# A mixture-of-experts weight ring: the first three tiles of each next unit are issued inside the running unit, and five tiles move back from idle arrays into the ring

## The reference, cut to what matters

```
logits = (xt @ w_router)
top_v, top_i = lax.top_k(logits, TOP_K)                  # TOP_K = 2
gate = sum(one_hot(top_i, N_EXPERTS) * softmax(top_v)[..., None], axis=1)
for e in range(N_EXPERTS):                               # 8 experts, D = 1024, D_FF_EXPERT = 2816
    out = out + gate[:, e:e+1] * ((silu(xt @ wg[e]) * (xt @ wu[e])) @ wd[e])
```

## Time and profile before

| | before |
|---|---|
| median of 3 runs | 1498.73 us (1493.27 to 1499.72) |
| the profiled execution, its own time | 1498.9 us |
| its span, first to last instruction | 1497.0 us |
| PE busy | 1433.6 us, 96% of the span |
| DVE, ACT busy | 529.7 us, 303.5 us |
| DMA, mean over the span | 276 GB/s |
| DMA in the experts' part | some 417 GB/s where it is busy throughout |
| chain that ended last | PE 91% |

### The profile page before, as it was taken

One profiled execution on the slowest core, in us unless ns is written; L12 is line 12 of the kernel. 1 busy time (PEld: TensorE's weight loads), 2 busy tenths in 40 slices (PEclk: granted clock), 3 DMA queues, 4 the chain that ended last, 5 costly groups with the idle time before them and its releaser, 6 DMA issues.

```text
span 1497.0 us, 60951 instructions
## 1 busy us (share of the span) xinstructions
PE 1433.6 (96%) x27147; PEld 1274.0 (85%) x27147; DVE 529.7 (35%) x1496; ACT 303.5 (20%) x870; POOL 38.7 (3%) x59
## 2 busy tenths in 40 slices
PE   5999999999999999999999899999999999999997
PEld 3888588999547787888778899999999999999896
DVE  1474427666636355788623210000101010010012
ACT  2112423000102523455342010100101010000101
POOL 0100000000000000100000000000000000000000
PEclk9999999999999999999999999999999999999999
DMA  9823849544448132100185999999999999999995
GB/s 390 321 95 123 308 170 396 196 170 169 179 180 330 57 127 87 35 8 7 48 283 219 378 397 403 417 417 418 399 418 399 419 417 417 417 403 417 394 414 212
DMA packets 77441, 413.76 MB, mean 276 GB/s; under 512 B 12920, under 2 KB 13354, under 8 KB 40452
## 3 DMA queue, kind: packets, MB, share of 16 engines
q1 hardware_dynamic: 68752, 399.96, 67.4%
q0 software_dynamic: 7456, 9.56, 2.2%
q10 hardware_dynamic: 1108, 2.41, 0.4%
HBM read 407.50 MB, written 6.48 MB: 277 GB/s over the span
## 4 chain that ended last, share of the span: by engine, by line
PE 91%; DVE 3%; DMA 2%; ACT 2%; issue 1%; ACTq 0%; DVEq 0%; SPq 0%
PE banks L1691 29%; PE banks L1715 14%; PE banks L1070 9%; PE banks L1109 4%; PE banks L718 3%; PE banks L721 3%; PE banks L824 3%; PE banks L827 3%; PE banks L1236 2%; PE banks L1295 2%; PE banks L744 2%; PE banks L1656 1%; PE banks L1313 1%; PE banks L860 1%; PE banks L1324 1%
## 5 line engine op out<-in xcount | busy, mean ns | idle before, releaser
L1691 PE MATMUL banks<-w,ring 128*64 128x86 f32 x11072 | 450.2, 238 | 8.1 <-issue 5.1
L1691 PEld LDWEIGHTS banks<-w,ring 128*64 128x64 f32 x11072 | 426.6, 136 | 18.9 <-issue 7.5
L3216 DVE TENSOR_TENSOR w<-w,banks 128x86 f32<-128x86 f32 x176 | 43.1, 245 | 566.5 <-PE banks L1691 558.4
L1715 PE MATMUL banks<-w,ring 128*64 128x86 f32 x5568 | 237.2, 238 | 1.7 <-issue 1.5
L1715 PEld LDWEIGHTS banks<-w,ring 128*64 128x64 f32 x5568 | 219.4, 137 | 2.0 <-issue 2.0
L2252 ACT ACTIVATE w<-banks 128x86 f32<-128x86 f32 x176 | 42.7, 242 | 587.7 <-PE banks L1691 587.7
L718 PE MATMUL banks<-w,ring 128*128 128x256 f32 x224 | 49.2, 380 | 0.6 <-issue 0.3
L744 PE MATMUL banks<-ring,ct 128*32 128x256 f32 x768 | 47.3, 395 | 2.3 <-ACT ct L1818 2.1
L721 PE MATMUL banks<-ring,w 128*128 128x256 f32 x224 | 48.9, 379 | 0.0
L718 PEld LDWEIGHTS banks<-w,ring 128*128 128x128 f32 x224 | 42.3, 190 | 7.4 <-issue 1.8
L721 PEld LDWEIGHTS banks<-ring,w 128*128 128x128 f32 x224 | 42.3, 190 | 5.9 <-DVE w L2334 0.2
(11 more groups left out here) (481 smaller groups left out, 1747.2 us busy)
## 6 DMA issues: line engine op xcount, KB each, us to landing
ring<-in_moe_gu SPq DMA_DIRECT2D x173, 1024.0 KB, 12.1
ring<-in_moe_w_down SPq DMA_DIRECT2D x174, 512.0 KB, 12.2
ring<-in_ada_w SPq DMA_DIRECT2D x48, 1024.0 KB, 5.2
ring<-in_ev_w_in SPq DMA_DIRECT2D x11, 1024.0 KB, 27.1
ring<-in_ffn_w_gate SPq DMA_DIRECT2D x11, 1024.0 KB, 12.4
ring<-in_ffn_w_up SPq DMA_DIRECT2D x11, 1024.0 KB, 10.8
ring<-in_ffn_w_down SPq DMA_DIRECT2D x11, 1024.0 KB, 6.4
ring<-in_ev_w_out SPq DMA_DIRECT2D x4, 1024.0 KB, 6.8
```

The lines of the kernel that those rows point to most:

```text
L1691: ins = [mm(b[hp, 0:CAP], w[:, k, hp], XG[:, k, :], start=k == 0, stop=k == KC - 1, skip_group_check=True) for hp in HALVES]
L1715: ins = [mm(bank[4 + c // 4][hp, (c % 4) * CAP:(c % 4 + 1) * CAP], w[:, c * P + hp.start:c * P + hp.stop], HIDU[:, t % 2, :], start=t == 0 ...
L3216: v.tensor_tensor(HIDU[:, t % 2, :], SILU[:, t % 2, :], bank[2 + t % 2][:, 0:CAP], ALU.mult).then_inc(sem("hid"), 1)
```

## The change

It has three parts. (1) SP's order: after d4, d5 and d6 of a unit, SP issues gu0, gu1 and d0 of the following unit, each behind a wait for the use of the same tile in the running unit. They no longer stand at the unit's end. Unit 7 issues none. (2) `AHEAD` is gone: in unit 0 the five tiles go through the ring like all others, and PE's unit 0 uses the same hardware loop as the others. (3) SP reads the running and the following unit's expert from the table `TBL` in each unit from 1 on; before, it did so only for the last.

```diff
-UNIT_TILES = [("gu", 0), ("gu", 1), ("d", 0)]
+FIRST_TILES = [("gu", 0), ("gu", 1), ("d", 0)]
+UNIT_TILES = []
...
+EARLY = {("d", ROWS): (("gu", 0), up_taken(0)), ("d", ROWS + 1): (("gu", 1), up_taken(1)),
+         ("d", ROWS + 2): (("d", 0), down_taken(0))}
...
-        AHEAD = {("gu", ROWS + 2 + n): W[6 + n][:, :] for n in range(3)}
-        AHEAD.update({("d", ROWS + 1 + n): W[9][:, n * D:(n + 1) * D] for n in range(2)})
...
-                    if u is None and (kind, b) in AHEAD:
-                        sp.wait_ge(sem("x"), 6)
-                        sp.dma_start(AHEAD[kind, b], src).then_inc(sem("x_in"), 16)
-                        continue
...
-            expert_tiles(None, 0)
-            with sp.Fori(1, NE - 1) as u:
-                expert_tiles(u, u)
+            def expert_tiles(u, e, following=None):
+
+                for kind, b in UNIT_TILES:
+                    expert_tile(kind, b, e, free_at(u, kind, b))
+                    if following is not None and (kind, b) in EARLY:
+                        first, taken = EARLY[kind, b]
+                        expert_tile(*first, following, u * UT + (N_MOE + taken))
+
+            for kind, b in FIRST_TILES:
+                expert_tile(kind, b, 0, free_at(0, kind, b))
+            expert_tiles(0, 0, 1)
             sp.wait_ge(sem("table"), 1)
-            with sp.Fori(NE - 1, sp.value_load(TBL[0:1, UNITS:UNITS + 1], min_val=NE, max_val=UNITS)) as u:
-                expert_tiles(u, sp.value_load(TBL[0:1, bass.ds(u, 1)], min_val=0, max_val=NE - 1))
+            last = sp.value_load(TBL[0:1, UNITS + 1:UNITS + 2], min_val=NE - 1, max_val=UNITS - 1)
+            with sp.Fori(1, last) as u:
+                expert_tiles(u, sp.value_load(TBL[0:1, bass.ds(u, 1)], min_val=0, max_val=NE - 1),
+                             sp.value_load(TBL[0:1, bass.ds(u + 1, 1)], min_val=0, max_val=NE - 1))
+            expert_tiles(last, sp.value_load(TBL[0:1, bass.ds(last, 1)], min_val=0, max_val=NE - 1))
...
-                if first_of_all:
-                    steps(0, False)
-                    steps(1, False, AHEAD)
-                with pe.Fori(2 if first_of_all else 0, LOOPS) as i:
-                    steps(i, True)
+                with pe.Fori(0, LOOPS) as i:
+                    for t in range(2, 2 + ROWS):
+                        gate_up(t, in_turn("gu", t, i))
+                        down(t - 1, in_turn("d", t - 1, i), u * HB + i * ROWS + (FT + t))
```

More of the change, by code:

```diff
@@ L135, in moe_slot, with moe_half, moe_landed @@
     return EXPERTS[2 if t in (0, HB - 1) else 4 + 2 * ((t - 1) % ROWS)]
+def moe_half(t):
+    return 1 if t == HB - 1 else 0
+def moe_landed(kind, t):
+    return "slot_last" if kind == "d" and t == HB - 1 else f"slot{moe_slot(kind, t)}"
 def moe_free(kind, t):
@@ L409, in program @@
         GT = PV[:, ADAB:ADAB + NST * NE].rearrange("p (s n) -> p s n", s=NST)
-        AHEAD = {("gu", ROWS + 2 + n): W[6 + n][:, :] for n in range(3)}
-        AHEAD.update({("d", ROWS + 1 + n): W[9][:, n * D:(n + 1) * D] for n in range(2)})
-        AHEAD_SLOTS = [moe_slot(kind, b) for kind, b in AHEAD]
-        AHEAD_LANDED = 16 * (2 + len(AHEAD))
         TBL = sb("tbl", [P, 16], I32)
@@ L598, in _, with expert_tile @@
-            expert_tiles(None, 0)
-            with sp.Fori(1, NE - 1) as u:
-                expert_tiles(u, u)
-            sp.wait_ge(sem("table"), 1)
-            with sp.Fori(NE - 1, sp.value_load(TBL[0:1, UNITS:UNITS + 1], min_val=NE, max_val=UNITS)) as u:
-                expert_tiles(u, sp.value_load(TBL[0:1, bass.ds(u, 1)], min_val=0, max_val=NE - 1))
+            def expert_tile(kind, b, e, at):
+                slot = ring[:, moe_slot(kind, b), :]
+                if kind == "gu":
+                    dst, src = slot, t["moe_gu"][bass.ds(e, 1), b].rearrange("a p n -> (a p) n")
+                else:
+                    dst = slot[:, moe_half(b) * D:(moe_half(b) + 1) * D]
+                    src = t["moe_w_down"][0][bass.ds(e, 1), b * P:(b + 1) * P, :].rearrange("a k n -> (a k) n")
+                sp.wait_ge(sem("tile_used"), at)
+                sp.wait_ge(sem("tile_used0"), at)
+                sp.dma_start(dst, src).then_inc(sem(moe_landed(kind, b)), 16)
@@ new lines, in _, with free_at @@
+            loaded = set()
+            def free_at(u, kind, b):
+                place = EXPERTS.index(moe_slot(kind, b)), moe_half(b) if kind == "d" else 0
+                if isinstance(u, int) and place not in loaded:
+                    loaded.add(place)
+                    return N_MOE + place[0] - RING + 1
+                return u * UT + (N_MOE + moe_free(kind, b))
+            def expert_tiles(u, e, following=None):
[4 more added lines that the diff above has]
+                        expert_tile(*first, following, u * UT + (N_MOE + taken))
@@ L1677, in _ @@
             gather(SEL0)
-            due0 = list(walk.due)
+            due0 = {f"slot{n}": landed for n, landed in enumerate(walk.due)}
+            due0.update(half0=0, half1=0, slot_last=0)
             def unit(u, prev=None, rows=False):
@@ L1693, in across, with gate_up @@
                     taken(ins)
[L1695 to L1702, removed]
+                def gate_up(t, due, between=lambda: None):
+                    pe.wait_ge(sem(moe_landed("gu", t)), due)
+                    w = ring[:, moe_slot("gu", t), :].rearrange("p (w k n) -> p w k n", w=2, k=KC)
                     across(bank[t % 2], w[:, 0])
@@ L1705, in gate_up, with down @@
                     across(bank[2 + t % 2], w[:, 1])
-                def down(t, arrived, due, hid, ahead=None):
-                    if ahead is None:
-                        pe.wait_ge(sem(arrived), due)
+                def down(t, due, hid):
+                    pe.wait_ge(sem(moe_landed("d", t)), due)
                     pe.wait_ge(sem("hid"), hid)
-                    half = D if t == HB - 1 else 0
-                    w = ring[:, moe_slot("d", t), half:half + D] if ahead is None else ahead
+                    w = ring[:, moe_slot("d", t), moe_half(t) * D:(moe_half(t) + 1) * D]
                     for c in range(KC):
@@ L1729, in outputs_turned, with once, in_turn @@
                     turn_y("y_turned")
-                def once(slot):
-                    return u * 16 + (due0[slot] + 16)
+                def once(kind, t):
+                    return u * 16 + (due0[moe_landed(kind, t)] + 16)
+                def in_turn(kind, t, i):
+                    return u * (16 * LOOPS) + i * 16 + (due0[moe_landed(kind, t)] + 16)
                 pe.wait_ge(sem("xg"), u * 2 + 2)
-                gate_up(0, once(moe_slot("gu", 0)), outputs_turned)
-                gate_up(1, once(moe_slot("gu", 1)))
-                down(0, f"slot{moe_slot('d', 0)}", once(moe_slot("d", 0)), u * HB + (FT + 1))
+                gate_up(0, once("gu", 0), outputs_turned)
+                gate_up(1, once("gu", 1))
+                down(0, once("d", 0), u * HB + (FT + 1))
                 if not first_of_all:
@@ L1746, in unit @@
                     slots(bank[6], SEL, TOKENS)
-                def due(slot, i, skipped):
-                    return u * (16 * LOOPS) + i * 16 + (due0[slot] + 16 - (16 if skipped and slot in AHEAD_SLOTS else 0))
-                def steps(i, skipped, ahead={}):
+                with pe.Fori(0, LOOPS) as i:
                     for t in range(2, 2 + ROWS):
[L1754 to L1757, removed]
-                if first_of_all:
-                    steps(0, False)
-                    steps(1, False, AHEAD)
-                with pe.Fori(2 if first_of_all else 0, LOOPS) as i:
-                    steps(i, True)
+                        gate_up(t, in_turn("gu", t, i))
+                        down(t - 1, in_turn("d", t - 1, i), u * HB + i * ROWS + (FT + t))
                 if not first_of_all:
@@ L1770, in unit @@
                     gather(SEL)
-                down(HB - 1, "slot_last", u * 16 + 16, u * HB + (FT + HB))
+                down(HB - 1, once("d", HB - 1), u * HB + (FT + HB))
             unit(0, rows=True)
```

## The result

The changed kernel takes 1503.18 us (median of 10 runs, 1501.44 to 1506.48), the kernel before 1498.25 us in the same comparison. The ratio is 1.0038, 95% interval 1.0026 to 1.0050: 4.9 us slower, which is more than the noise (the interval leaves out 1) and within the 0.5% that the prediction counted as no change. The profiled execution took 1501.4 us, with a span of 1499.6 us against 1497.0.

What follows compares the result with a forecast made beforehand. Two nearly equal limits, 82.9 us of DMA and 83.0 us of PE a unit, with the scatter deciding. +8.1 (units 1 to 6) - 3.5 (unit 7) - 1.5 (unit 0) = +3.1 on 1498.9 gave 1502 us, range 1489 to 1512.

Steps and rivals of the forecast that it cites:

- the path from the pause to PE's wait for gu8: After SP's 13.7 us issue pause the queue runs low; gu8 lands after 12.5 us, one more than PE allows.
- units 1 to 6: Units 1, 4 and 6 each lengthen by the scatter's 2.8 us, units 2, 3 and 5 stay: +8.1 us.
- unit 7: The last unit issues no early tiles, so has 6.3 us less to load: 88.25 to 84.8 us, -3.5 us.
- unit 0: PE still sets the pace; one loop copy in place of three drops a wait for code: -1.5 us.
- table reads: SP's reads in units 1 to 6 cost nothing, as over 10 us of loads are queued then.
- No unit keeps a reserve that outlasts the scatter: DMA meets each turn with nothing in hand, so each unit with a scatter waits: 85.7 us.
- the queue idles some 0.7 us at the turn: After the change the DMA queue runs empty before gu6, where before it never did after unit 1.
- The scatter's price: One scatter that counts in full makes a unit 2.8 us longer than its tiles need; bounds 0 and 5.6.
- The bound taken from PE: Unit 7 on PE alone: 83.0 less the turn's 2.2 plus 3 us of waits for code, about 84 us.
- Rival 2: Loads only move, the scatter counts in some units as now; only -3.5 and -1.5 stay: 1494 us, chance 0.2.
- Rival 3: Idle time at each turn takes the scatter in, no unit pays: 1486 us, chance 0.15.
- Rival 4: Scatter meets early tiles, costs 5.6 us in units 1 to 6; sign gu6 landing after over 9 us: 1519 us, 0.15.

Runs made afterwards that it cites:

- experiment 8: The changed kernel with SP taking the unit's number as the expert in units 1 to 6, without the table reads; 1504.55 us, ratio 1.0043.
- experiment 1: The changed kernel with a scatter of 2 rows in place of 86; 1486.86 us, ratio 0.9929.
- experiment 2: The kernel before with a scatter of 2 rows in place of 86; 1483.06 us, ratio 0.9904.
- experiment 10: The changed kernel with gu0, gu1 and d0 of the next unit all behind d4 and a scatter of 2 rows; 1482.01 us, ratio 0.9897.
- experiment 3: The changed kernel with the three early tiles issued at the unit's end again, behind d21; 1494.43 us, ratio 0.9979.
- experiment 9: The changed kernel with gu0, gu1 and d0 of the next unit all behind d4, ahead of gu6, full scatter; 1503.56 us, ratio 1.0042.
- experiment 4: The changed kernel with only gu0 of the next unit behind d4, gu1 and d0 behind d21; 1494.56 us, ratio 0.9980.

## Why the prediction was right

1502 us was forecast and 1503.2 us measured. The kind of each term was right, and the path from the pause to PE's wait for gu8 showed step by step; that the sum came within 1.2 us is luck, as the table shows. The terms, in the profiled executions:

| term | predicted, us | measured, us |
|---|---|---|
| units 1 to 6 | +8.1 | +10.9 (506.4 to 517.3) |
| unit 7 | -3.5 | -6.4 |
| unit 0 | -1.5 | -1.2 (89.71 to 88.47) |
| table reads | 0 | none that shows (experiment 8; the intervals are +-1.9 us) |
| sum | +3.1 | +2.6 in the spans (0.7 of it an earlier start of unit 0), +4.9 in the medians |

Units 1 to 6 lost 2.8 us more than forecast and unit 7 won 2.9 us more, and the two misses cancel.

- *No unit keeps a reserve that outlasts the scatter.* Right: gu8 lands after 12.7 us (12.5 forecast), PE waits 1.01 us for it (one forecast).
- *Units 1 to 6.* Right in kind, 2.8 us too small. The prediction worked out that the queue idles some 0.7 us at the turn and left it out of its sum. It measures 1.0 us a unit (experiments 1, 2 and 10). The scatter's price beside it is then 2.5 us, not 2.8.
- *Unit 7.* The size was off by 2.9 us. The bound taken from PE, about 84, held 3 us of waits that the prediction took for waits for code (1.41 and 1.53 us before, ended by nothing that the profile shows). In the changed kernel's unit 7 PE waits once, 1.25 us, and that for a tile. Why the other waits are gone was not tried. The prediction also passed over the clock, which reads 0.98 for unit 7 in the earlier trace rows. Before, PE waits 2.27 us for a tile in unit 7, and then the granted clock is 0.50 for some 3 us and a block takes 4.25 us in place of 2.61. This is that block in the kernel before:

```profile
1435.71 4.25 PE L1691 MATMUL banks<-w,ring 128*64 128x86 f32 x64 [2.27 <-DMA ring<-in_moe_gu]
```

In the changed kernel the clock stays at 1.00 throughout unit 7. The queues were busy in that stretch (share 1.02), so how much of the 6.4 us is the clock's was not separated.
- *Unit 0.* The sum was right, the account of it only roughly: two waits of 1.12 and 1.13 us are there, earlier than before, and PE never waited for a tile. The prediction's own figure for gu21, 11.7 us, lay above the 11.5 that PE allows.
- *Rival 2 (the loads only move)* falls with units 1 to 6, 10.9 us longer, and experiment 3 puts that down to the place of the three tiles. *Rival 3 (the pause takes in the scatter)* falls with the 2.5 us that stay. *Rival 4 (each scatter costs 5.6 us)* is shown by no kernel; the most is 3.6 us a unit, in experiment 9, where gu6 lands after 10.3 us, past the 9 us that the prediction named as its sign.

**What stays open.** The same scatter costs a unit 2.8 us or nearly nothing before the change, 1.1 to 3.0 us in experiments 3 and 4, 2.5 in the changed kernel and 3.6 in experiment 9. Before the change it is 1.6 us on the mean ((506.4 - 6 x 82.8) / 6). The prediction put the difference down to work in hand at the turn. Experiment 9 was to give the queue that work and did not, so it tests this neither way. The rows there fit engines that are unevenly late, as a scatter on two of them would leave them, but no row names a single engine. Why a unit pays or does not pay is argued and not shown.

## What to carry to other kernels

When two limits stand within 0.1% of each other (82.9 us of DMA and 83.0 us of PE a unit), a small third load decides, and it is found by cutting the trace into repeats and asking why some are longer. Moving a load earlier does not add time to the queue. For it to win anything it must fall where the queue would idle, and not ahead of a tile that is wanted sooner; experiment 9 shows that even then it need not win. Choose the number of rows of an indirect DMA by its divisors: 96 in place of 86 won more (some 15 us in the changed kernel) than any order of the tiles (9 us), and 8 us in the kernel before.

## What the runs showed of the hardware

- The number of rows of GpSimd's indirect DMA, by its divisors up to 16, sets how it disturbs a stream of loads: 83 rows cost the changed kernel 45 us more than 86 rows, 96 rows cost it 15 us less (1548.5, 1503.2 and 1488.6 us).
- Its packets on queue q0 are 16 times one more than the rows of an engine: 1344, 704, 112 and 32 for 83, 86, 96 and 2 rows.
- Engines need not keep step: in experiment 9 half of the engines' time is idle at 975 to 976 us, while a tile issued 11 us before is still to land 2 us later.
- GpSimd's own time to issue it goes by the rows of an engine and not by bytes: 1.95 us for 83 rows, 1.40 for 86, 0.90 for 96 and 0.85 for 2, so some 11 to 14 ns for each row of an engine (an estimate from 1947, 1402, 902 and 847 ns and 83, 43, 6 and 1 rows). The rows of the three kernels in that order (86 rows from the changed kernel), duration in ns as min/median/max:

```profile
L704 POOL DMA_INDIRECT sums<-w,slot_row x7: 1942/1947/2017, 890.3 to 1446.1; - x7
```

```profile
L704 POOL DMA_INDIRECT sums<-w,slot_row x7: 1401/1402/1476, 888.8 to 1406.0; - x7
```

```profile
L704 POOL DMA_INDIRECT sums<-w,slot_row x7: 898/902/955, 889.6 to 1392.7; - x7
```
